# The first loads of a two-stage sequence model on one core: weights and input in halves, in the order in which they are used

## The reference, cut to what matters

```python
def rms_norm(x, g):
    xf = x.astype(jnp.float32)
    xf = xf * lax.rsqrt(jnp.mean(xf * xf, axis=-1, keepdims=True) + EPS)
    return (xf * g).astype(x.dtype)

def swiglu(x, w_gate_up, w_down):
    gate, up = jnp.split(x @ w_gate_up, 2, axis=-1)
    return (jax.nn.silu(gate) * up) @ w_down

x = x + FFN_HALF * swiglu(rms_norm(x, ffn1_norm[l]), ffn1_w_gate_up[l], ffn1_w_down[l])
```

## Time and profile before

| | |
|---|---|
| time of three runs | 1806.51, 1808.74, 1809.49 us; median 1808.74 |
| time of the profiled execution | 1808.37 us |
| its span in the profile | 1806.5 us |
| PE busy | 1736.2 us, 96% of the span |
| weight loads (PEld) | 1621.6 us, 90% |
| DVE, ACT, POOL busy | 1252.2, 889.3, 358.7 us |
| DMA | 282.86 MB, 157 GB/s in the mean |
| first matmul | 12.15 us after the start of the span |

### The profile page before, as it was taken

One profiled execution on the slowest core, in us unless ns is written; L12 is line 12 of the kernel. 1 busy time (PEld: TensorE's weight loads), 2 busy tenths in 40 slices (PEclk: granted clock), 3 DMA queues, 4 the chain that ended last, 5 costly groups with the idle time before them and its releaser, 6 DMA issues.

```text
span 1806.5 us, 35596 instructions
## 1 busy us (share of the span) xinstructions
PE 1736.2 (96%) x15296; PEld 1621.6 (90%) x15296; DVE 1252.2 (69%) x2101; ACT 889.3 (49%) x1566; POOL 358.7 (20%) x308
## 2 busy tenths in 40 slices
PE   7999999999899999999999999989999999989997
PEld 6999988887799998999998888789999888879987
DVE  5876665866567776687676676656777665779974
ACT  5564435323345654566443533334655545556652
POOL 3552000000112651156200000011265200121110
PEclk9999999999799999999999999979999999989999
DMA  8655522211147565565562221014555542335442
GB/s 302 237 218 193 212 94 94 89 33 46 48 160 256 210 238 185 207 258 202 196 228 73 99 90 48 25 48 165 223 225 214 195 180 105 117 132 183 175 154 104
DMA packets 44492, 282.86 MB, mean 157 GB/s; under 512 B 6064, under 2 KB 6704, under 8 KB 17712
## 3 DMA queue, kind: packets, MB, share of 16 engines
q1 hardware_dynamic: 44336, 280.60, 42.7%
HBM read 279.53 MB, written 1.05 MB: 155 GB/s over the span
## 4 chain that ended last, share of the span: by engine, by line
PE 83%; DVE 11%; ACT 3%; issue 1%; DMA 1%; POOL 0%; SPq 0%; DVEq 0%; ACTq 0%
PE bank L489 16%; PE bank L491 15%; PE bank L490 15%; PE bank L497 10%; PE bank L985 7%; PE bank L498 5%; PE bank L1581 4%; DVE WL L480 2%; ACT WH L475 2%; PE bank L527 1%; PE bank L1848 1%; PE bank L1125 1%; DVE XC L1054 1%; DMA ring<-wst 1%; PE bank L1858 1%
## 5 line engine op out<-in xcount | busy, mean ns | idle before, releaser
L489 PE MATMUL bank<-XNH,WH 128*128 128x256 f32 (+1 forms) x2176 | 621.7, 286 | 17.7 <-DVE XNL L573 12.2
L480 DVE TENSOR_TENSOR WL<-ring,WH 128x2048 fp32r<-128x2048 f32 (+1 forms) x235 | 508.6, 2167 | 166.8 <-ACT WH L475 166.5
L491 PE MATMUL bank<-XNH,WL 128*128 128x256 f32 (+1 forms) x2176 | 617.2, 284 | 0.0
L490 PE MATMUL bank<-XNL,WH 128*128 128x256 f32 (+1 forms) x2176 | 615.2, 283 | 0.0
L475 ACT ACTIVATE WH<-ring 128x2048 fp32r<-128x2048 f32 (+1 forms) x235 | 405.5, 1729 | 217.4 <-PE bank L491 152.7
L489 PEld LDWEIGHTS bank<-XNH,WH 128*128 128x128 f32 x2176 | 413.5, 190 | 23.7 <-DVE XNL L573 12.4
L490 PEld LDWEIGHTS bank<-XNL,WH 128*128 128x128 f32 x2176 | 415.1, 191 | 0.0
L491 PEld LDWEIGHTS bank<-XNH,WL 128*128 128x128 f32 x2176 | 414.8, 191 | 0.0
L497 PE MATMUL bank<-HP,WH 128*128 128x512 f32 x770 | 267.6, 392 | 0.8 <-POOL HP L882 0.7
L498 PE MATMUL bank<-HP,WL 128*128 128x256 f32 x770 | 215.4, 280 | 0.0
L985 PE MATMUL bank<-XN,ring 128*128 128x256 f32 x832 | 200.3, 389 | 0.0
(11 more groups left out here) (474 smaller groups left out, 2615.3 us busy)
## 6 DMA issues: line engine op xcount, KB each, us to landing
ring<-wst SPq DMA_DIRECT2D x206, 1024.0 KB, 4.8
ring<-wst SPq DMA_DIRECT2D x80, 704.0 KB, 4.1
LP<-lp SPq DMA_DIRECT2D x1, 1872.0 KB, 7.0
LP<-lp SPq DMA_DIRECT2D x1, 1792.0 KB, 8.6
X<-xin SPq DMA_DIRECT2D x2, 512.0 KB, 4.5
out<-X SPq DMA_DIRECT2D x4, 256.0 KB, 2.5
C<-cst SPq DMA_DIRECT2D x1, 193.0 KB, 10.6
AL<-cst SPq DMA_DIRECT2D x1, 192.0 KB, 10.6
```

The costliest lines, as they stand in the source:

```text
L480: e.do.tensor_tensor(WL[:, slot[q], 0:n], ring[:, i % NSLOT, 0:n], WH[:, slot[q], 0:n].bitcast(F32), ALU.subtract).then_inc(*w_dve.up("low ...
L489: e.do.matmul(o, WH[:, s, cols], xh, start=first, stop=False)
L490: e.do.matmul(o, WH[:, s, cols], xl, start=False, stop=False)
L491: return e.do.matmul(o, WL[:, s, cols], xh, start=False, stop=last)
```

## The change

SP issues block 0 and X in halves: first half of block 0, first half of X, the norm's weights (LP from n1 on), second half of block 0, second half of X. The first half of block 0 has a semaphore of its own (s_w), the halves of X have one each, and the second half of block 0 counts on the slot's. ACT and DVE wait for a half only. The constants C 0:256 go behind block 2. All later DMAs keep their order; there is one issue more than before.

```diff
-        s_c, s_c2, s_x, s_v, s_lp, s_sp, s_out = (sem(n) for n in ("s_c", "s_c2", "s_x", "s_v", "s_lp", "s_sp", "s_out"))
+        s_c, s_c2, s_v, s_lp, s_sp, s_out, s_w = (sem(n) for n in ("s_c", "s_c2", "s_v", "s_lp", "s_sp", "s_out", "s_w"))
+        s_x = [sem(f"s_x{i}") for i in range(2)]
...
         def act_begin(e):
             for half in range(2):
                 at = slice(1024 * half, 1024 * half + 1024)
-                e.wait_ge(*landed(0))
+                e.wait_ge(*(landed(0) if half else (s_w, 16)))
                 e.do.activation(WH[:, 0, at], ring[:, 0, at], ACT.Copy).then_inc(*w_act.up("high", 0, half))
-                e.wait_ge(s_x, 32)
+                e.wait_ge(s_x[half], 16)
                 e.wait_ge(s_v, 16)
...
         def dve_begin(e):
...
-                e.wait_ge(s_x, 32)
+                e.wait_ge(s_x[half], 16)
...
         def sync(e):
-            for n in range(2):
-                e.do.dma_start(X[:, 4 * n:4 * n + 4, :], xin[:, 4 * n:4 * n + 4, :]).then_inc(s_x, 16)
-            e.do.dma_start(C[:, 0:256], cst[:, 0:256]).then_inc(s_c, 16)
-            e.do.dma_start(LP[:, LC["n1"]:LN], lp[0, :, LC["n1"]:LN]).then_inc(s_v, 16)
-            for i in range(len(plan)):
+            for half in range(2):
+                at = slice(1024 * half, 1024 * half + 1024)
+                e.do.dma_start(ring[:, 0, at], wst[0, :, at]).then_inc(s_slot[0] if half else s_w, 16)
+                e.do.dma_start(X[:, 4 * half:4 * half + 4, :], xin[:, 4 * half:4 * half + 4, :]).then_inc(s_x[half], 16)
+                if half == 0:
+                    e.do.dma_start(LP[:, LC["n1"]:LN], lp[0, :, LC["n1"]:LN]).then_inc(s_v, 16)
+            for i in range(1, len(plan)):
                 if i == NSLOT:
+                    e.do.dma_start(C[:, 0:256], cst[:, 0:256]).then_inc(s_c, 16)
                     e.do.dma_start(C[:, 256:CC["gs"]], cst[:, 256:CC["gs"]]).then_inc(s_c2, 16)
```

## The result

The changed kernel takes 1811.76 us (median of 10 runs, 1809.68 to 1813.55), the kernel before 1806.19 (10 runs, 1803.08 to 1809.49). The ratio is 1.0031, with a 95% interval of 1.0021 to 1.0040: slower by 3.8 to 7.2 us. The profiled execution has a span of 1809.4 us. PE runs the same matmuls in the same order in both programs, so one of them serves as a ruler for the first 140 us: the last group of the small matmuls on AD in the first feed-forward part starts at 139.51 before and at 144.25 after, 4.7 us later. From there on the two programs are the same; their spans differ by 2.9 us, so the rest of these two executions took 1.8 us less after than before.

A forecast was written before the change was run, and what follows sets the result against it. The prediction took PE as bound by the start of block 3, set by block 4's landing in a full DMA stream. Landing 0, SP and C 0 and clock 1.7 on 1808.37 gave 1810.1, as a median 1810.4; range 1806.0 to 1813.0.

The forecast's parts named there:

- The sum: Whole kernel: landing 0, SP and C 0, clock 1.7 us on the profiled 1808.37; as a median, 1810.4.
- the early ones: Signs at the kernel's start: first matmul between 7.2 and 8.7 us, block 1 at 16 to 17.
- Loads and start: First blocks: with halved, reordered loads PE starts at about 7.7, 4.4 us earlier; block 2 ends at 28.8.
- Nothing of it reaches the end: Before block 3: PE's 3.9 us gain goes into a 5.3 us wait while the rows come at 34.09.
- Value for the move of block 4's landing: DMA stream up to block 4: landing unmoved, 0; bounds 3.9 us earlier and 0.4 later.
- C behind block 2: cost 0: Constants' load: lands at about 15, before the sums after block 1 need it near 21.8; cost 0.
- The clock: PE behind the rows: clock falls in the 5.3 us gap, half pace for 3.75 us, loss 1.7, bounds 0 and 4.6.
- The 10.2 us of the stretch from 452 to 464: Low-clock stretch later in the kernel before, used for the clock loss's upper bound of 4.6 us.
- the first (nothing): Whole kernel: clock does not fall or PE does not start as early, so 1808.7 us; chance 0.19.
- the second (faster): Block 4 lands as much earlier as it is issued, 3.9 us reach the end, 1804.8 us; chance 0.08.
- The third rival: Behind the rows: clock stays low for 10.2 us, 4.6 us lost, 1813.3 us; chance 0.10.
- the last item of the chances: DMA stream: block 4's landing moves by 0.5 to 3 us; chance 0.08, put within 0.2% apart from small edges.

The follow-up runs named there:

- third run: Changed kernel with DVE's inverse root moved ahead of the low parts of blocks 3 and 4; ratio 0.9984 to the kernel before.
- fifth run: Changed kernel with PE's first matmul also waiting for block 2 to land, every DMA in its place; ratio 1.0008 to the kernel before.
- e7: Kernel before with 40 small one-column matmuls on the constants ahead of PE's first real one, loads unchanged; ratio 1.0055.
- e11: Changed kernel without C's move: block 0 and X in halves, C 0:256 ahead of block 1; ratio 1.0025 to the kernel before.
- first run: Changed kernel, but SP issues block 5 only when block 4 has landed; ratio 1.0027 to the kernel before.
- second run: Changed kernel with 54 unused 256-column matmuls on PE between block 2 and the rows; ratio 1.0008 to the kernel before.
- sixth run: Kernel before, loads unchanged, with DVE's inverse root moved ahead of the low parts of blocks 3 and 4; ratio 0.9987.

## Why the prediction came out as it did

The sign was right, and so were two parts of the mechanism: nothing of the early start reaches the end, and the clock falls in the gap. The third part, that block 4 lands where it did, was wrong, and so was the size: 1.7 us forecast, 5.6 measured (3.8 to 7.2). The time of 1811.76 lies in the range of 1806.0 to 1813.0, but that is in part luck. The sum started from 1808.74, the median of three runs; the median of ten is 1806.19. The measured 5.6 us on top of 1808.74 would be 1814.3, outside the range. By the prediction's own mark of 0.2% the result, 0.31% (0.21 to 0.40%), counts as slower, which had a chance of 0.13. Of its signs the early ones held; the landing of block 4 (26.5 to 27.5), the rows (33.7 to 34.6), the gap (4 to 6) and the slow stretch behind it (2 to 4) all came out above their bounds, at 29.0, 36.17, 6.70 and 5.9. Step by step:

- *Loads and start:* right. PE at 7.84 (forecast 7.7), ACT's first WH at 5.08 (4.95), block 1 at 16.86 (16.1 to 17), block 2's end at 29.5 (28.8).
- *Nothing of it reaches the end, since the rows hang on block 4:* right. It is the same chain, and the third run turns the loss into a gain by cutting that link alone.
- *Value for the move of block 4's landing: 0, bounds 3.9 earlier and 0.4 later:* this is the step that failed. It moved by 2.1 later. The argument, that block 4 "stands behind the same 9.18 MB", counted the bytes and took the stream as one pipe. It is 16 engines, and a block lands with the slowest. One part is the single late engine: 1.5 us between the fifteenth and the sixteenth (27.54 and 29.03), and block 4 lands 1.4 us earlier when PE alone is moved (fifth run). The other, 0.6 to 0.7 us, stays with the loads. From 2 to 26 us the stream made 369 GB/s instead of 380, which is 0.26 MB or 0.7 us. It is lost early, under the loads in halves: block 1 has landed at 12.14 instead of 11.84 although the 128 KB of C (0.3 us) no longer stand in front of it, and SP2, once C has gone through as well, at 22.60 instead of 22.01. (Block 1: 11.96 to 12.14 in the six traces with the changed loads, 11.84 to 11.89 in four of the five with the loads of before and 12.12 in the fifth, e7.) With the halves and C in its old place (e11) block 1 landed at 12.76.
- *C behind block 2: cost 0:* wrong by itself (1.0016; of the 1.4 us by which block 4 landed later, one late engine took 1.0 and C's place the rest), right about the sums, which never waited for C.
- *The clock:* the fall was right, at 5.9 us of work against the 3.75 taken from the start; it cost 2.7 us instead of 1.7, within the bounds of 0 and 4.6. The 10.2 us of the stretch from 452 to 464 were the length of the low clock here too (31.9 to 42.1); the prediction counted them from the rows on, but 4.3 of them lay in the gap.
- Landing 2.1 and clock 2.7 make 4.8, against the ruler's 4.7 and the runs' 5.6 (3.8 to 7.2).

The rivals: the first (nothing) and the second (faster) did not happen. The second leant on a row misread: the block of 4.7 us in the earlier trace rows, issued at 28.8, did have a block in front of it, which was issued at 25.2 and landed 5.2 us later, at 30.4. A block with nothing in front is block 5 of the first run, issued at 28.9 after block 4 had landed: it took 4.9 us. The estimate of 4.4 us from the Trainium skill (DMA: Bandwidth & Descriptors, Anatomy of one DMA), which the page fits for DMAs that GpSimd issues, comes near that 4.9; behind the full stream a block took 12.2. The third rival was right that slower beyond 0.2% was possible, but not by its path: nearly half of it came from the landing. What happened to the landing is the last item of the chances, a move by 0.5 to 3 us, which had 0.08. The advice of the Trainium skill against long gaps between bursts of matmuls in mid-kernel (TensorE: Matmul & The Clock Gate, Why this matters for your kernels) is borne out: filling the gap in the second run gave 2.7 us back.

**What stays open.** The trace has no number for the DMA engine of a packet. That the late engine is the one that took the fetch is read from times: one engine of 16 is behind exactly where the fetch began before its engine can have closed the block, its closing packet in the sixth run falls on the end of the fetch, and moving PE moves both. No run changed the fetch with PE's work untouched. Why it starts when it does is known only roughly: with PE's first matmul at 7.8 to 8.0 it came anywhere from 22.6 to 25.4. A fetch takes 0.9 to 1.1 us and its engine is up to 1.6 us late; the rest was not explained. Nor was the cause of the 0.6 to 0.7 us that the loads in halves cost by block 1.

## What to carry to other kernels

Before you bring the start forward, look at what the first common wait hangs on. If that is a load in a full stream, an earlier start only makes the gap longer, and the gap costs the clock too: find the link (here DVE's program order) and cut it first. And a full DMA stream is not one pipe: count a block as landed when the last of its DMA engines is done, and ask what else those engines carry.

## What the runs showed of the hardware

- One 16 KB instruction packet appears in the first 30 us of each trace, and its start follows PE: 23.0 us with PE's first matmul at 7.84, 27.9 with 14.62, both with the same loads. If it starts before its DMA engine has closed its share of a block, that block's semaphore counts the sixteenth engine 1.0 to 1.6 us after the fifteenth (0.8 in e11); if it starts behind it, 0.0 to 0.2 us.
- After a gap of 6.70 us, in which the granted clock fell to 0.50, 5.9 us of dense matmuls ran at 0.21 us each before the pace was 0.12 again (4.6 in the first run, behind 6.65 us), against 3.75 us at the start of the kernel before. 54 matmuls that nobody needs, in the gap, avoid it.
- 17.23 us of matmuls of one column at the start did not bring the pace up: PE's dense matmuls behind them, from 23.7 us on, stood 0.21 us apart until 28.7.
- A float32 matmul of one column with a weight load of 128x128 took 0.43 us at the slow pace (40 in 17.23 us), and shows as two.
